# A fused decoder kernel whose first layer takes raw x into its projections and applies the norm behind them

## The reference

```
proj = rms(x) * g @ w_in               # 1024 -> 6144: q, k (1024 each), v, gate (2048 each)
q, k = theta_shift(q), theta_shift(k)  # a rotation by position
o    = retention(q, k, v)              # 4 heads; o_t = sum_{s<=t} gamma^(t-s) (q_t . k_s) v_s
x    = x + (rms(o) * silu(gate)) @ w_out
```

## Time and profile before

| | |
|---|---|
| time of the runs | 2070.24 us median of 3 (2069.32 to 2070.68) |
| profiled execution, first to last instruction (its own time shown) | 2066.5 us span |
| TensorE busy | 1981.1 us, 96% |
| VectorE busy | 1434.1 us, 69% |
| GpSimd busy | 884.6 us, 43% |
| ScalarE busy | 473.6 us, 23% |
| granted TensorE clock, mean over the span | 0.992 |

### The profile page before, as it was taken

The page is one execution under the profiler, slowest core; times in us unless marked ns, Lnnn a source line. Parts: engine busy times, 40 slices in busy tenths (PEclk is TensorE's granted clock), DMA queues, the critical chain, the costliest instruction groups (busy, mean ns, idle before and its releaser), DMA issues.

```text
span 2066.5 us, 27516 instructions
## 1 busy us (share of the span) xinstructions
PE 1981.1 (96%) x10152; PEld 1462.9 (71%) x10152; DVE 1434.1 (69%) x3059; ACT 473.6 (23%) x998; POOL 884.6 (43%) x653
## 2 busy tenths in 40 slices
PE   7999999999999999999989999999999999999996
PEld 6888876878788985688876666666666666766663
DVE  3673124333352666647999999899989989987767
ACT  4122223123552325732222010100101010010000
POOL 4354432427302652422524455454554544454332
PEclk9999999999999999999999999999999999999998
DMA  9565422515301321114448999999999999999997
GB/s 252 166 217 192 144 89 92 191 54 173 92 2 44 98 71 51 42 62 154 133 185 344 422 421 422 421 417 418 421 419 416 413 415 422 402 421 415 422 422 245
DMA packets 92627, 527.08 MB, mean 255 GB/s; under 512 B 10048, under 2 KB 14576, under 8 KB 42992
## 3 DMA queue, kind: packets, MB, share of 16 engines
q1 hardware_dynamic: 49680, 246.95, 32.2%
q0 software_dynamic: 37440, 270.55, 32.1%
q10 hardware_dynamic: 5408, 8.34, 1.9%
HBM read 518.46 MB, written 7.34 MB: 254 GB/s over the span
## 4 chain that ended last, share of the span: by engine, by line
PE 46%; DMA 28%; DVE 16%; POOL 5%; issue 3%; ACT 1%; SPq 0%; POOLq 0%; DVEq 0%; ACTq 0%
PE ps L827 29%; DMA ring<-in_peer_uv,consts 14%; DMA work<-in_peer_uv,consts 13%; PE ps L1131 5%; DVE tables L2039 3%; POOL ring L2592 2%; POOL work L2592 2%; DVE work L2014 2%; DVE ring L2014 2%; PE ps L914 2%; PE ps L856 1%; PE ps L971 1%; PE ps L778 1%; DVE hT L2039 1%; PE ps L903 1%
## 5 line engine op out<-in xcount | busy, mean ns | idle before, releaser
L1225 PE MATMUL ps<-work,tmp 128*128 128x512 f32 x1008 | 450.4, 600 | 25.2 <-DVE tmp L2064 25.0
L1200 PE MATMUL ps<-hT,work 128*128 128x256 f32 x2048 | 465.9, 381 | 0.0
L2511 POOL TENSOR_TENSOR w_lo<-ring,w_hi 128x1024 fp32r<-128x1024 f32 (+2 forms) x116 | 275.0, 2375 | 398.0 <-ACT w_hi L2132 397.8
L1200 PEld LDWEIGHTS ps<-hT,work 128*128 128x128 f32 x2048 | 385.0, 190 | 76.1 <-issue 29.6
L1225 PEld LDWEIGHTS ps<-work,tmp 128*128 128x128 f32 x1008 | 191.5, 192 | 250.5 <-issue 215.4
L2592 POOL DMA_INDIRECT ring<-in_peer_uv,consts x128 | 233.4, 1824 | 259.5 <-DVE tables L2039 231.3
L2592 POOL DMA_INDIRECT work<-in_peer_uv,consts x128 | 227.0, 1773 | 267.1 <-DVE tables L2039 216.3
L827 PE MATMUL ps<-w_hi,x_hi 128*128 128x512 f32 (+2 forms) x544 | 208.8, 384 | 1.5 <-DVE tmp L1562 1.1
L2132 ACT ACTIVATE w_hi<-ring 128x1024 fp32r<-128x1024 f32 (+2 forms) x116 | 120.4, 1041 | 385.1 <-PE ps L827 278.6
L827 PE MATMUL ps<-w_lo,x_hi 128*128 128x512 f32 (+2 forms) x544 | 207.3, 381 | 0.0
L2014 DVE CUSTOM_DVE_ANT_0 ring<-ring,tables 128x1024 f32<-128x1024 f32 x128 | 155.5, 1224 | 46.0 <-DMA ring<-in_peer_uv,consts 45.0
(11 more groups left out here) (347 smaller groups left out, 3009.2 us busy)
## 6 DMA issues: line engine op xcount, KB each, us to landing
work<-in_u_steps SPq DMA_DIRECT2D x64, 1024.0 KB, 9.0
work<-in_peer_v SPq DMA_DIRECT2D x64, 1024.0 KB, 9.0
ring<-in_a_w_in SPq DMA_DIRECT2D x48, 512.0 KB, 4.5
ring<-in_ada_w SPq DMA_DIRECT2D x48, 512.0 KB, 5.0
ring<-in_peer_w_q SPq DMA_DIRECT2D x32, 512.0 KB, 3.4
ring<-in_a_w_out SPq DMA_DIRECT2D x16, 512.0 KB, 4.1
ring<-in_b_w_in SPq DMA_DIRECT2D x16, 512.0 KB, 4.1
ring<-in_c_in SPq DMA_DIRECT2D x12, 512.0 KB, 3.7
```

The costliest lines, as they stand in the source:

```text
L1200: mm = pe.matmul(ps[:, 4 + s, j * DT:(j + 1) * DT], u_ring[:, s, j, k, :], hT[:, k, GATHERED * P:T], start=(k == 0), stop=(k == KD - 1))
L1225: mm = pe.matmul(ps[:, 2 * t + half, :], tmp[:, s, j * DT + t * P:j * DT + (t + 1) * P], v_ring[:, s, j, half * BANK:(half + 1) * BANK], s ...
L2511: pool.tensor_tensor(w_lo[q % NPIECE][:, 0:n], ring[:, at:at + n], w_hi[q % NPIECE][:, 0:n], ALU.subtract).then_inc(w_split, 1)
```

## The change

Raw x goes into the projections. The token's factor r = 1/rms is applied where a token lies along the partitions: on ScalarE's evictions of v and gate, on VectorE's evictions of the scores (the factor of the key token), in the square of the outputs, and by one more GpSimd multiplication on their inverse root (the factor of the query token). q and k stay raw. TensorE's transposes wait for x's landing alone. x lands in the place where its scaled copy stood.

SP issues the first weight piece and the identity ahead of x. ScalarE splits one piece before x_hi and one after each second bank of it; behind x_hi it issues the seven constants, squares x, and does SiLU of c. GpSimd splits four pieces before the inverse roots of x. The bias matmul and VectorE's two instructions on it stand behind the first projection, and ScalarE issues the store of the table behind the splits for the second.

The diff, without the renumbering of semaphores that follows from it (in the other layers' transposes and in one wait of ScalarE):

```diff
@@ -141,10 +141,11 @@
         jobs.add("xT_a", k)
-    jobs.add("bias", 0)
     for n in range(12):
...
             jobs.add("a_in", n, i)
+        if n == 0:
+            jobs.add("bias", 0)
         if ADA_LAG <= n < ADA_IN_A + ADA_LAG:
@@ -444,7 +445,8 @@
         a_sT = hT[:, :, :].rearrange("p (b j) t -> p b j t", b=2)
-        a_xn = W(8192, NT, D)
+        a_x, a_sq = W(8192, NT, D), W(16384, NT, D)
+        r_tok = astat[:, 7, 0:NT]
@@ -685,13 +688,21 @@
         def _(sp):
+            def load_piece(c):
...
+                at = c % NPIECE * PIECE
+                sp.dma_start(ring[:, at:at + pieces[c].src.shape[1]], pieces[c].src).then_inc(piece_loaded[c % NPIECE], 16)
...
+            load_piece(0)
+            sp.dma_start(ident[:], ins["ident"]).then_inc(const_loaded, 16)
             for t in range(NT):
-                sp.dma_start(xres[:, t, :], ins["x"][t * P:(t + 1) * P, :]).then_inc(x_loaded[t], 16)
+                sp.dma_start(a_x[:, t, :], ins["x"][t * P:(t + 1) * P, :]).then_inc(x_loaded[t], 16)
                 if t == 0:
-                    sp.dma_start(ident[:], ins["ident"]).then_inc(const_loaded, 16)
                     sp.dma_start(cols[:], ins["cols"]).then_inc(const_loaded, 16)
...
                 name = piece.name
+                if c == 0:
+                    continue
                 if name == ("a_in", 1, 0):
@@ -703,8 +714,7 @@
                         full(sp, *before.last)
-                at = c % NPIECE * PIECE
-                sp.dma_start(ring[:, at:at + piece.src.shape[1]], piece.src).then_inc(piece_loaded[c % NPIECE], 16)
+                load_piece(c)
                 if name == ("pq", 0, 0):
@@ -790,9 +800,9 @@
                         if k == 0:
-                            pe.wait_ge(xn_done, NT * n + t + 1)
+                            ready(t)
                         one(k, t)
-                pe.wait_ge(xn_done, NT * n + NT)
+                ready(NT - 1)
                 for k in range(KD):
@@ -883,15 +893,16 @@
             pe.wait_ge(const_loaded, 32)
-            stream_transposes("xT_a", a_xn, 0)
-            o = start("bias", 0)
-            pe.wait_ge(row_loaded, 16 * 7)
-            end(pe.matmul(o[0:SWA_H, 0:384], bias_w, bias_hot, start=True, stop=True), "bias", 0)
-            pe.wait_ge(made, 1)
+            stream_transposes("xT_a", a_x, lambda t: pe.wait_ge(x_loaded[t], 16))
             for n in range(12):
...
                         ready=[lambda k: pe.wait_ge(x_high, k + 1), lambda k: drained(pe, "xT_a", k)])
+                if n == 0:
+                    o = start("bias", 0)
+                    pe.wait_ge(row_loaded, 16 * 7)
+                    end(pe.matmul(o[0:SWA_H, 0:384], bias_w, bias_hot, start=True, stop=True), "bias", 0)
+                    pe.wait_ge(made, 1)
                 if ADA_LAG <= n < ADA_IN_A + ADA_LAG:
@@ -1326,20 +1337,12 @@
-            for t in range(NT):
-                stream_norm(0, a_xn, t)
             dve.wait_ge(const_loaded, 32)
...
                                                ALU.subtract), "xT_a", k)
-            o = full(dve, "bias", 0)
-            dve.wait_ge(row_loaded, 16 * 7)
-            dve.tensor_tensor(bias_mask, o[0:SWA_H, 0:384], bias_mask, ALU.add).then_inc(bias_done, 1)
-            dve.wait_ge(bias_done, 1)
...
-            taken(dve.tensor_scalar(bias_mask, bias_mask, float(SWA_D ** 0.5), None, ALU.mult), "bias", 0)
             dve.wait_ge(silu_c, 1)
@@ -1363,19 +1366,26 @@
                                           ALU.add).then_inc(qk_done, 1)
+                if n == 0:
+                    o = full(dve, "bias", 0)
+                    dve.wait_ge(row_loaded, 16 * 7)
+                    dve.tensor_tensor(bias_mask, o[0:SWA_H, 0:384], bias_mask, ALU.add).then_inc(bias_done, 1)
+                    dve.wait_ge(bias_done, 1)
+                    taken(dve.tensor_scalar(bias_mask, bias_mask, float(SWA_D ** 0.5), None, ALU.mult), "bias", 0)
                 if 1 <= n <= ADA_IN_A:
...
             ada(ADA_IN_A)
+            dve.wait_ge(rr_done, NT)
             for h in range(RET_H + 1):
...
                             full(dve, "ret_o", h - 2, NT - 1)
-                        taken(dve.tensor_tensor(a_sT[:, h % 2, j, 0:T - j * P], o[:, 0:T - j * P],
-                                                decay[:, h, 0:T - j * P], ALU.mult), "ret_s", h, j)
+                        taken(dve.scalar_tensor_tensor(a_sT[:, h % 2, j, 0:T - j * P], o[:, 0:T - j * P], r_tok[:, j:j + 1],
+                                                       decay[:, h, 0:T - j * P], ALU.mult, ALU.mult), "ret_s", h, j)
                 if h >= 1:
@@ -2109,14 +2119,6 @@
-            act.dma_start(rows[:], ins["rows"]).then_inc(row_loaded, 16)
-            act.dma_start(iota[:], ins["iota"]).then_inc(row_loaded, 16)
-            act.dma_start(causal, ins["causal"]).then_inc(row_loaded, 16)
-            act.dma_start(trig[:], ins["trig"]).then_inc(row_loaded, 16)
-            act.dma_start(bias_w, ins["rel_bias"]).then_inc(row_loaded, 16)
-            act.dma_start(bias_hot, ins["bias_hot"]).then_inc(row_loaded, 16)
-            act.dma_start(bias_mask, ins["bias_mask"]).then_inc(row_loaded, 16)
...
             split_n = [0]
@@ -2143,25 +2145,40 @@
-            stream_squares(0, a_xn, lambda t: act.wait_ge(x_loaded[t], 16))
             act.wait_ge(const_loaded, 32)
-            high_parts(NPIECE)
+            high_parts(1)
             for k in range(KD):
...
                 act.activation(x_hi[:, k, :], o, ACT.Copy, scale=col("a_g", k)).then_inc(x_high, 1)
+                if k % 2:
+                    high_parts(min(k // 2 + 2, NPIECE))
+            act.dma_start(bias_w, ins["rel_bias"]).then_inc(row_loaded, 16)
+            act.dma_start(bias_hot, ins["bias_hot"]).then_inc(row_loaded, 16)
+            act.dma_start(bias_mask, ins["bias_mask"]).then_inc(row_loaded, 16)
+            act.dma_start(rows[:], ins["rows"]).then_inc(row_loaded, 16)
+            act.dma_start(iota[:], ins["iota"]).then_inc(row_loaded, 16)
+            act.dma_start(causal, ins["causal"]).then_inc(row_loaded, 16)
+            act.dma_start(trig[:], ins["trig"]).then_inc(row_loaded, 16)
+            for t in range(NT):
+                act.wait_ge(x_loaded[t], 16)
+                act.activation(a_sq[:, t, :], a_x[:, t, :], ACT.Square, accum_out=stat[:, 0, t:t + 1]).then_inc(sq_done, 1)
             act.activation(csil[:], col("c", 0, KD), ACT.Silu).then_inc(silu_c, 1)
...
-            drained(act, "bias", 0)
-            act.dma_start(ins["bias_rows"].rearrange("p h u -> h p u"),
-                          bias_mask.unsqueeze(1).to_broadcast([SWA_H, P, 384])).then_inc(bias_kept, 16)
             for n in range(12):
                 high_parts_for("a_in", n, 3)
+                if n == 1:
+                    drained(act, "bias", 0)
+                    act.dma_start(ins["bias_rows"].rearrange("p h u -> h p u"),
+                                  bias_mask.unsqueeze(1).to_broadcast([SWA_H, P, 384])).then_inc(bias_kept, 16)
+                if n == RET_H:
+                    act.wait_ge(rr_done, NT)
                 for t in range(NT) if n >= RET_H else ():
                     o = full(act, "a_in", n, t)
+                    r = r_tok[:, t:t + 1]
                     if n < 2 * RET_H:
-                        taken(act.activation(a_v[:, t, (n - 4) * BANK:(n - 3) * BANK], o, ACT.Copy), "a_in", n, t)
+                        taken(act.activation(a_v[:, t, (n - 4) * BANK:(n - 3) * BANK], o, ACT.Copy, scale=r), "a_in", n, t)
                     else:
-                        taken(act.activation(a_z[:, t, (n - 8) * BANK:(n - 7) * BANK], o, ACT.Silu), "a_in", n, t)
+                        taken(act.activation(a_z[:, t, (n - 8) * BANK:(n - 7) * BANK], o, ACT.Silu, scale=r), "a_in", n, t)
             high_parts(split_at["a_out", 0, 0] + NPIECE)
@@ -2171,7 +2188,8 @@
                         act.wait_ge(qk_done, 16)
-                    act.activation(tmp[:, u % 2, :], o, ACT.Square, accum_out=rstat[:, 0, u:u + 1]).then_inc(z_sq, 1)
+                    act.activation(tmp[:, u % 2, :], o, ACT.Square, scale=r_tok[:, i:i + 1],
+                                   accum_out=rstat[:, 0, u:u + 1]).then_inc(z_sq, 1)
             for f in range(RET_K):
@@ -2483,10 +2501,11 @@
                     pool.wait_ge(sq_done, NT * n + i + 1)
-                    if n >= 1:
-                        pool.wait_ge(xn_done, NT * (n - 1) + t + 1)
+                    if n >= 2:
+                        pool.wait_ge(xn_done, NT * (n - 2) + t + 1)
                     at = slice(t, t + 1)
-                    rsqrt(stat[:, 0, at], stat[:, 1, at], stat[:, 2, at], 1, D, ms_done, NT * n + i + 1, rr_done)
+                    rsqrt(stat[:, 0, at], stat[:, 1, at], r_tok[:, at] if n == 0 else stat[:, 2, at], 1, D,
+                          ms_done, NT * n + i + 1, rr_done)
@@ -2512,11 +2531,15 @@
+            low_parts(NPIECE)
             stream_rsqrt(0)
...
```

(18 more changed lines are left out.)

## The result

| | before | after |
|---|---|---|
| median of 5 runs each, side by side | 2069.43 us (2069.24 to 2070.68) | 2081.95 us (2080.95 to 2084.88) |
| ratio of the times | | 1.0059, 95% interval 1.0048 to 1.0071 |
| span of the profiled execution | 2066.5 us | 2083.0 us |
| TensorE busy | 1981.1 us | 1987.1 us |
| granted clock, mean | 0.992 | 0.986 |

I had forecast 2073.5, with a range up to 2078.0. The profiled execution of after is its slowest; the other four have spans of 2079.2 to 2080.4, so a thing in it that is worth under 4 us proves little.

A forecast was written before the change was run, and what follows sets the result against it. TensorE was taken as the bound: time it won or lost ahead of 100 us carries to the end. Front -4.5, held loads +7.3 and +0.3, retention +0.2 made +3.3 on 2070.24: 2073.5 us, range 2065.0 to 2078.0.

The forecast's parts named there:

- If it stands still again, they land 22.2 and 24.7 us behind 55.4: Third projection: loads (ada 0, 2) and (2, 3), counted from the store's issue, land at 77.6 and 80.1; TensorE waits 7.3 us.
- A: The forecast itself: the front's gain is there and the moved store gives it back; 2073.5 us (2071.5 to 2075.5), chance 0.56.
- Nothing, and 17 us: Bounds of TensorE's 7.3 us wait at the third projection; 17 if both loads stood still for the store's whole 34.5 us.
- rival C: The fourth load, piece (3, 0), is served only at the store's end; TensorE waits 3.7 us more, 2077.2 us; chance 0.11.
- The front gain: Program start: first projection at 15.5 instead of 20.9, 5.35 us sooner; 4.5 us net of the bias matmul, bounds 2.4 and 5.3.
- ScalarE's row of work: Behind x_hi: issues, splits, squares and SiLU last to 32.4, then piece (1, 0) is split; 2.0 us to spare, cost nothing.
- rival D: ScalarE's work behind x_hi ends later than 34.4 and TensorE waits at the second projection; 2075.5 us or more; chance 0.05.
- Piece (3, 0): The fourth load held by the store: lands at 85.3, split by 89.0, where TensorE asks at 90.0.
- my 0.3: Microseconds added to the sum for piece (3, 0), the fourth load held, as its split was near the edge.
- Rival B: Loads aren't held, or share the DMA engines with the store; 2067.4 to 2068.6 us, 2066.2 with no cost; chance 0.28.
- Turns between queues: If each DMA engine takes store and load packets in turn, the sum has about 1 us in place of 7.3.
- Retention: Added score factor and GpSimd multiplication: TensorE's 64 transposes wait for banks VectorE frees, 0.2 us, bounds 0 and 0.4.

The follow-up runs named there:

- e4: The changed kernel with the store of the bias table issued three splits sooner, behind the split of piece (1, 3): 2075.55 us, ratio to before 1.0022.
- e7: The changed kernel with rows of 768 bytes in place of 1536 for 127 of the store's 128 copies: 2068.92 us, one run.
- e1: The changed kernel with one copy of the bias table stored in place of 128: 2065.94 us, ratio to before 0.9981.
- e5: The changed kernel with bias constants and matmul at the start, and the store ahead of the other four constants on ScalarE's queue: 2077.54 us, ratio to before 1.0037.
- e8: The changed kernel with the store issued one split sooner, behind the split of piece (2, 1): 2081.66 us, ratio to before 1.0054.
- e9: The changed kernel with bias matmul before the first projection, four constants ahead of the store, store ahead of the second projection's splits: 2065.75 us, ratio to before 0.9978.

## Why the prediction was wrong, point by point

- **The step that failed** is "If it stands still again, they land 22.2 and 24.7 us behind 55.4". It carried over a landing measured from the store's issue, and so took for granted that the store releases the other queue at a fixed age. The first load is held from its own issue (table above): (ada 0, 2) landed 29.3 us behind the store's issue and (2, 3) 31.8, at 86.09 and 88.63. The same rows give the right number so: the earlier trace rows has 17.5 us from issue to landing for the load issued first; 66.4 + 17.5 = 83.9, one more piece 2.6, the split 3.7, so 90.2 - 76.5 = 13.7 us of wait where I wrote 7.3, and 13.7 were measured. (The step of 2.6 for the second load is from the same rows; it was 2.54 in after.) One store with loads at 5 and 10 us behind it was all I had, I named that against A, and my loads were at 11; I should have carried both ways of counting as bounds. "Nothing, and 17 us" did hold it, yet the range's upper end (2078) came from rival C and not from this bound.
- **The clock behind the wait** was no term of the sum: 13.7 us without matmuls, then half clock from 81 to 98, which made most of the 2.9 us lost on matmuls. In e4 a wait of 6.4 us was followed by 10.2 us of half clock too. So a long wait of TensorE has a price beside its own length.
- **The front gain** was right in kind, too large in size: 3.44 and 2.6 net, not 5.35 and 4.5. The third tile landed at 10.52 and not at 9.4 (1.1 us): SyncE's queue had moved the 2.22 MB by 8.5 us, as I assumed, but the landing came 2 us behind that and not 1. The delay isn't firm: in e7, with the same loads in the same order, the tile landed at 9.51, 1.0 us behind. And the 23 transposes took 5.18, not 4.4 (0.8 us): the earlier trace rows has 4.61 for them, and I went below it on the strength of a mean. In six other kernels with the same order of loads (e1, e4, e5, e7, e8, e9) the first projection started at 16.45 to 17.36, so 17.45 is the latest seen; none came near 15.5. The 1.64 us from x_hi to the first matmul were 1.68.
- **ScalarE's row of work** behind x_hi: right that it costs nothing, no wait near 38 us (rival D wrong), but it was shorter than I had it. The seven DMA issues ran beside the ACTIVATEs, from 16.75 to 20.2, and not between them; the split of (1, 0) began at 28.9 and not at 32.4.
- **Piece (3, 0)**, rival C and my 0.3: wrong, it landed at 92, later than C's 90, but behind its one wait TensorE asked for the piece only at 101, so it was in time. **Rival B**, shared DMA engines: wrong, q1 moved 0.01 MB in 13.8 us.
- **Turns between queues**: in the five traces of the table, the DMA engines moved some 55 rows each, on average, between a new load's issue and its first packet; then both queues moved (106 packets of q10 beside 85 of q1 from 82 to 84 in after). The Trainium skill (DMA: Bandwidth & Descriptors, "Queues, rings and completion order") says that a DMA engine takes packets from its queues in turn; if a row of the profile is such a packet, the traces agree for the second stretch and not for the first.
- **Retention**: 0.2 us forecast; after is 12.9 us behind before at its start and at its transposes alike, so the trace shows no cost.
- **Sum**: -2.5 + 13.7 + 2.9 = +14.1 at the fourth projection instead of +3.3; 12.5 in the medians.

## What to carry to other kernels

A large store like this one (3 MB in rows of 1.5 KB, 34.5 us) is no background work: put it where no load issued during its life is one that an engine is short of; that it was hidden in the old place says nothing of the new one. When a stall is carried from one place to another, ask from which event it counts, and price both answers. If the price reaches a stall of TensorE, add the half clock behind it. Check what follows on the queue of a store as well: issues behind it stop the engine that makes them. Rows of another size for as large a store weren't tried.

## What the runs showed of the hardware that I had not expected

- The first load on SyncE's queue that meets ScalarE's store with more than 875 rows left waits for 874 to 878 of them (55 per DMA engine on average, 13.5 us), at 4 to 17 us behind the store's issue alike; with 620 (e4) or 710 (e7) left, nearly all go first. The first load's issue took 0.33 us, the next three 4.4 us each in after.
- The store moves 0.1 MB per us with rows of 1536 B and of 768 B, with the DMA engines shown busy to 0.9; SyncE's queue alone moved 0.41 to 0.44 MB per us from 12 to 16 us in after.
- Four small loads behind the store on one queue hold the issuing engine for 10.70, 5.37, 4.10 and 2.67 us (e5).
- A wait of TensorE of 13.7 us came with 17 us at the 1.2 GHz level, waits of 6.4 us (e4) and 9.6 us (e5) with 10.2 us; the fall lies within the wait, and the matmuls behind it ran at the lower level at first.
